# A two-block transformer kernel on one core: two further 2 MB weight slots for the expert stages, taken from double buffers and from the scratch of dynamic transfers

## What is computed

```
pg = softmax(h @ router_g);  gi = argmax(pg)              # one of 4 groups
le = (h @ router_e).reshape(t, 4, 8) of group gi
pk, ik = top_k(softmax(le), 2)                            # two experts of 8 in the group
weight = pg[gi] * pk / sum(pk);  expert = gi * 8 + ik
y[token] += weight * ((silu(x @ w1[e]) * (x @ w3[e])) @ w2[e])   # 32 experts, w1, w3: 1024 x 512, w2: 512 x 1024
x = x + gate * y
```

## Time and profile before

| | us |
|---|---|
| median of three runs (2308.2 to 2309.95) | 2309.11 |
| span of the profiled execution, first to last instruction | 2304.8 |
| median less span | 4.3 |
| PE busy in that span | 2107.9 (91%) |
| PE idle before the UP1 and UP3 products, released by a weight transfer, both layers | 56.3 |
| layer 0 expert stage on PE | 1194.5 to 1656.8 |
| layer 1 expert stage on PE | 1819.8 to 2282.5 |

### The profile page before, as it was taken

The page is one execution under the profiler, slowest core; times in us unless marked ns, Lnnn a source line. Parts: engine busy times, 40 slices in busy tenths (PEclk is TensorE's granted clock), DMA queues, the critical chain, the costliest instruction groups (busy, mean ns, idle before and its releaser), DMA issues. The chain is left out here.

```text
span 2304.8 us, 25911 instructions
## 1 busy us (share of the span) xinstructions
PE 2107.9 (91%) x10718; PEld 1359.1 (59%) x10718; DVE 623.4 (27%) x1420; ACT 461.7 (20%) x899; POOL 252.8 (11%) x385
## 2 busy tenths in 40 slices
PE   8999899999999998878889998888889899998897
PEld 6854587678878755667674443333478644333334
DVE  4566340232213235743231110011111311111101
ACT  2222231222213345444320000000111200000001
POOL 2034120111112133000100000000000001000000
PEclk9999999999999999989889999999899899999998
DMA  7479644334432221110269999999924699999994
GB/s 251 146 325 412 249 146 146 109 128 146 146 99 73 74 73 37 37 38 2 110 248 380 428 428 427 427 427 428 380 100 154 280 379 427 428 428 427 428 428 188
DMA packets 105042, 575.51 MB, mean 250 GB/s; under 512 B 5536, under 2 KB 28665, under 8 KB 75225
## 3 DMA queue, kind: packets, MB, share of 16 engines
q1 hardware_dynamic: 103455, 570.59, 61.6%
q10 hardware_dynamic: 970, 2.23, 0.3%
q0 software_dynamic: 496, 0.97, 0.2%
HBM read 572.72 MB, written 1.05 MB: 249 GB/s over the span
## 5 line engine op out<-in xcount | busy, mean ns | idle before, releaser
L3094 PE MATMUL ex_u<-ring,ex_xt 128*64 128x512 f32 x1024 | 235.1, 614 | 29.2 <-DMA ring<-in_w 27.8
L3094 PE MATMUL ex_u<-ring_extra,ex_xt 128*64 128x512 f32 x1024 | 233.5, 610 | 28.5 <-DMA ring_extra<-in_w 28.5
L784 PE MATMUL linear_ps<-hT,ring 128*128 128x256 f32 x960 | 211.8, 383 | 8.5 <-PEq L444 6.4
L784 PEld LDWEIGHTS linear_ps<-hT,ring 128*128 128x128 f32 x960 | 184.4, 193 | 35.5 <-issue 8.5
L3094 PEld LDWEIGHTS ex_u<-ring,ex_xt 128*64 128x64 f32 x1024 | 82.6, 141 | 178.2 <-issue 178.1
L3094 PEld LDWEIGHTS ex_u<-ring_extra,ex_xt 128*64 128x64 f32 x1024 | 80.5, 141 | 178.7 <-issue 178.1
L2151 PE MATMUL dl_front<-dn_src,ring 128*128 128x256 f32 (+1 forms) x512 | 176.5, 501 | 2.4 <-DVE dp_cv L2318 2.4
L3200 DVE TENSOR_TENSOR ex_hid<-ex_sil,ex_u 128x512 f32<-128x512 f32 x32 | 34.8, 1086 | 490.0 <-PE ex_u L3094 490.0
L1570 PE MATMUL ffn_ps<-hT,ring 128*128 128x256 f32 x704 | 153.9, 382 | 4.3 <-PEq L677 4.3
L1570 PEld LDWEIGHTS ffn_ps<-hT,ring 128*128 128x128 f32 x704 | 134.9, 192 | 23.3 <-issue 4.7
L2151 PEld LDWEIGHTS dl_front<-dn_src,ring 128*128 128x128 f32 x512 | 99.4, 199 | 65.1 <-issue 57.6
(11 more groups left out here) (617 smaller groups left out, 2679.5 us busy)
## 6 DMA issues: line engine op xcount, KB each, us to landing
ring_extra<-in_w SPq DMA_DIRECT2D x88, 2048.0 KB, 25.4
ring<-in_w SPq DMA_DIRECT2D x88, 2048.0 KB, 25.5
ring<-in_ada_w SPq DMA_DIRECT2D x16, 2048.0 KB, 15.9
ring<-in_ffn_w_up SPq DMA_DIRECT2D x22, 1024.0 KB, 6.5
ring<-in_w_in SPq DMA_DIRECT2D x8, 2048.0 KB, 9.2
ring<-in_ada_w SPq DMA_DIRECT2D x16, 1024.0 KB, 14.7
ring<-in_w_in_a SPq DMA_DIRECT2D x8, 2048.0 KB, 8.5
ring<-in_w SPq DMA_DIRECT2D x16, 1024.0 KB, 7.2
```

The costliest lines, as they stand in the source:

```text
L784: mm = pe.matmul(ps[:, q % banks, 0:n], w[:, k, j * P:(j + 1) * P], src[:, k, 0:n], start=k == 0, stop=k == kc - 1)
L3094: mm = pe.matmul(u[H * a:H * a + H, i, :], xt[:, b, k, H * a:H * a + H], cols, start=k == 0, stop=k == KC - 1, skip_group_check=True)
```

## The change

1. `LATE = 2`: two more slots, ten in all, in the expert stages only. `late_slots` allocates them inside `stage_experts`, so their first tiles can be issued once that stage has begun. The list of slots for the experts goes round ten slots in place of eight.
2. SBUF for them: `xt`, `give`, `back`, `ys` get one buffer each; `sil` goes (silu is written into `hid`, in the order that the transposes read, and the multiply works on `hid` in place); `iota` is 128 wide and not 512; `pick` holds two tiles of 128 and not all four, and DVE subtracts 128 from `route_at` ahead of a further tile.
3. With single buffers some waits move: POOL waits for UP3 of the pair before (it was the one before that); ACT's silu waits for the transposes of the pair before; DVE makes the next pair's `give` right after the turned `give`, and copies `back` only after Y0.
4. `dynamic_dma_scratch_size=1024`: POOL's scratch for transfers is cut, and POOL's small loads move to SP, ahead of the weight tiles that SP issues in those two stages.

```
-        self.slots = RING + EXTRA
+        self.slots = RING + EXTRA + LATE
+    def late_slots(self, ctx):
+        for i in range(LATE):
+            self.ring[RING + EXTRA + i] = self.sb(f"ring_late{i}", [P, SLOT], ctx=ctx)
...
         @block.sync
         def _(sp):
+            if loads:
+                loads(sp)
             K.issue(sp, g0 + tiles)
...
-            pool.dma_start(ld[:, :], io["ssm_log_dt"][0]...)          # and four more, now sp.dma_start in start_loads
-        pool.dma_start(S["wg"][:, :, :], w)                           # and six more, now sp.dma_start in start_loads
...
-                elif at < RING + EXTRA:
+                elif at < K.slots:
                     slot = at
                 else:
-                    slot = min(range(RING + EXTRA), key=lambda i: K.latest[i])
+                    slot = min(range(K.slots), key=lambda i: K.latest[i])
...
-        iota = K.sb("ex_iota", [P, 2 * T], ctx=st)
-        pick = K.sb("ex_pick", [P, TT, 2 * T], ctx=st)
+        K.late_slots(st)
+        iota = K.sb("ex_iota", [P, P], ctx=st)
+        pick = K.sb("ex_pick", [P, 2, TT, P], ctx=st)
-        give = K.sb("ex_give", [P, 2, TT, 2, H], ctx=st)
-        xt = K.sb("ex_xt", [P, 2, KC, 2 * H], ctx=st)
-        sil = K.sb("ex_sil", [P, 512], ctx=st)
+        give = K.sb("ex_give", [P, TT, 2, H], ctx=st)
+        xt = K.sb("ex_xt", [P, KC, 2 * H], ctx=st)
-        back = K.sb("ex_back", [P, 2, T], ctx=st)
-        ys = K.sb("ex_ys", [P, 2, D], ctx=st)
+        back = K.sb("ex_back", [P, T], ctx=st)
+        ys = K.sb("ex_ys", [P, D], ctx=st)
...
-                if p >= 2:
-                    pool.wait_ge(full.sem, step(p - 2, UP3))
+                pool.wait_ge(full.sem, step(p - 1, UP3))
...
-                    act.wait_ge(hidden.sem, hidden.at(p))
-                act.activation(sil[:, :], u[:, 0, :], ACT.Silu)
+                    act.wait_ge(turned.sem, turned.at(p))
+                act.activation(hid[:, :].rearrange("s (k q) -> s q k", k=fc), u[:, 0, :].rearrange("s (q k) -> s q k", k=fc), ACT.Silu)
...
-    nc = bacc.Bacc("TRN2", target_bir_lowering=False, num_devices=1)
+    nc = bacc.Bacc("TRN2", target_bir_lowering=False, num_devices=1, dynamic_dma_scratch_size=1024)
```

More of the change, by code:

```diff
@@ L109, in __init__ @@
         self.own = {n: Counter(ctx.enter_context(nc.semaphore(f"{n}_own_step"))) for n in ("dve", "act", "pool")}
-        self.ring = [self.sb(f"ring{i}", [P, SLOT]) for i in range(RING)] + [None] * EXTRA
+        self.ring = [self.sb(f"ring{i}", [P, SLOT]) for i in range(RING)] + [None] * (EXTRA + LATE)
     def unique(self, name):
@@ L154, in no_extra_slots @@
     def no_extra_slots(self):
-        self.ring[RING:] = [None] * EXTRA
+        self.ring[RING:] = [None] * (EXTRA + LATE)
+    def late_slots(self, ctx):
+        for i in range(LATE):
+            self.ring[RING + EXTRA + i] = self.sb(f"ring_late{i}", [P, SLOT], ctx=ctx)
     def issue(self, sp, done, until=None):
@@ L746, in stage_linear_renorm, with linear_stage @@
     K.used = g0 + (4 if fill else 2)
-def linear_stage(K, src, n_chunks, evac, kc=KC, per_tile=4, n=T, beside=None, token_major=()):
+def linear_stage(K, src, n_chunks, evac, kc=KC, per_tile=4, n=T, beside=None, token_major=(), loads=None):
     nc = K.nc
@@ L1054, in cosines, with start_loads @@
         act.activation(S["cos"][:, :, :], rot[:, :, :], ACT.Sin, scale=turn).then_inc(waved.sem, waved.tick())
+    def start_loads(sp):
+        sp.dma_start(ld[:, :], io["ssm_log_dt"][0].rearrange("(i h) -> i h", h=2)).then_inc(loads.sem, loads.tick())
+        for j, n in enumerate(("ssm_b_re", "ssm_b_im")):
+            sp.dma_start(br[:, j], io[n][0].rearrange("g s c -> (g s) c").rearrange("(i q) c -> q i c", q=P)).then_inc(loads.sem, loads.tick())
+        for j, n in enumerate(("ssm_c_re", "ssm_c_im")):
+            sp.dma_start(cr[:, j], io[n][0].rearrange("g c s -> (g c) s").rearrange("(b r) s -> r b s", r=P)).then_inc(loads.sem, loads.tick())
+    S["start_loads"] = start_loads
     def programs(block):
@@ L1734, in evac @@
                     return act.activation(proj[:, c, :], ps, ACT.Sigmoid, bias=K.col("b_gate", c - 16))
-                linear_stage(K, K.hT, 32, evac, token_major=(2,), beside=lambda st: ssm_params(K, S, st))
+                linear_stage(K, K.hT, 32, evac, token_major=(2,), beside=lambda st: ssm_params(K, S, st),
+                             loads=lambda sp: S["start_loads"](sp))
                 K.ada["ps"], K.ada["t_ps"] = K.ps("ada_ps", [P, 512], banks), K.ps("ada_t", [P, 512], banks)
@@ L1947, in program @@
                 w = io[n][l].rearrange("(k p) n -> p k n", p=P)
-                pool.dma_start(K.routers[:, l, :, c:c + w.shape[2]], w).then_inc(loads.sem, loads.tick())
+                sp.dma_start(K.routers[:, l, :, c:c + w.shape[2]], w).then_inc(loads.sem, loads.tick())
+    def program(pool):
         own = K.own["pool"]
@@ L3026, in _ @@
                     for i, part in enumerate((sorted_lo, sorted_hi)):
-                        ins = pool.tensor_copy(xt[:, p % 2, 4 * i:4 * i + 4, H * a:H * a + H], part[:, :, bass.ds(start, H)])
+                        ins = pool.tensor_copy(xt[:, 4 * i:4 * i + 4, H * a:H * a + H], part[:, :, bass.ds(start, H)])
                 ins.then_inc(windowed.sem, windowed.tick())
@@ L3179, in make_give @@
                         e = 2 * p + a
-                        ins = dve.tensor_scalar(give[:, p % 2, t, a, :], iota[:, 0:H], R["place"][:, t, e:e + 1], R["weight"][:, t, e:e + 1],
+                        ins = dve.tensor_scalar(give[:, t, a, :], iota[:, 0:H], R["place"][:, t, e:e + 1], R["weight"][:, t, e:e + 1],
                                                 ALU.is_equal, ALU.mult)
@@ L3204, in _ @@
                 dve.wait_ge(given_turned.sem, given_turned.at(p + 1))
-                dve.tensor_copy(back[:, p % 2, :], g_ps[:, 0:T]).then_inc(back_moved.sem, back_moved.tick())
+                if p + 1 < pairs:
+                    make_give(p + 1)
                 if p + 2 < tiles:
                     make_pick(p + 2)
-                if p + 2 < pairs:
-                    make_give(p + 2)
+                dve.wait_ge(full.sem, step(p, Y0))
+                dve.tensor_copy(back[:, :], g_ps[:, 0:T]).then_inc(back_moved.sem, back_moved.tick())
                 dve.wait_ge(full.sem, step(p, Y1))
-                dve.tensor_copy(ys[:, p % 2, 512:1024], u[:, 1, :]).then_inc(y1_moved.sem, y1_moved.tick())
+                dve.tensor_copy(ys[:, 512:1024], u[:, 1, :]).then_inc(y1_moved.sem, y1_moved.tick())
             for c in range(KC):
```

59 lines of the change are left out of this document (31 added, 28 removed).

## The result

The changed kernel took a median of **2283.36 us** (four runs, 2281.46 to 2292.64) against 2308.65 us for the kernel before on the same chip: a ratio of 0.9897, 95% interval 0.9875 to 0.992. Five further runs of the same kernel gave 2284.98 us, 0.9909 [0.9895, 0.9924].

A forecast was written before the change was run, and what follows sets the result against it. The prediction took the expert stages' weight stream as the bound. Two slots save 2 x 9.8 = 19.6 us, other terms 0: span 2304.8 to 2285.2 us, plus 4.3 gives a median of 2289.5 us; 8-in-10 range 2285.6 to 2299.

The forecast's parts named there:

- The bound: In both expert stages weight transfers at 427 to 428 GB/s set the pace; PE is faster by 4.3 us a pair.
- The two slots: At each expert stage's start two more tiles fill 9.8 us of idle transfer time; each stage ends 9.8 us earlier.
- second gap in layer 0: Idle transfers from 1225 to 1231, 5.3 us; 2.8 us of it would be filled, its end set by PE.
- The marker for PE's waits: PE's wait for tiles over both layers would fall from 56.3 us by somewhat under 20 us.
- Phase of the end: A slower product group after idling may fall behind a stage's last tile: 1.7 us either way per layer, 3.4 us in all.
- The first wait: PE's first wait for a tile in an expert stage would come about two pairs later (9.8 / 4.3).
- The single buffers: POOL, DVE and ACT steps in the expert pairs stay covered by other work; 0 to 1.0 us in all, taken as 0.
- The small loads on SP: S5 tables queued among SP's first weight tiles: between -0.5 and +14.4 us, taken as 0; delta and router loads cost nothing.
- Rival A: Small tables in SP's queue stall PE before the S5 products by up to 14.4 us: up to 2303.9 us; chance 0.12.
- lower bound of -0.5 us: Best case for moving the S5 tables to SP's queue: PE's 0.49 us wait before the S5 products is gone.
- the sum: Both expert stages' gains, -2 x 9.8 = -19.6 us, taken off the 2304.8 us span: 2285.2 us; median 2289.5 us.
- the rest behind the last awaited tile: PE work at each expert stage's end, claimed unchanged, so each stage ends the full 9.8 us earlier.

The follow-up runs named there:

- e_sb8: The changed kernel with LATE = 0 (eight slots), all other edits kept, against the kernel before: median 2305.39 us, ratio 0.9985 [0.9972, 0.9998].

## Why the forecast was right in sign and too high in time

**The bound** held: 426 to 428 GB/s in both stages, PE waits for tiles to the last or last but one pair. The 358 GB/s that the Trainium skill gives for one core ("DMA: Bandwidth & Descriptors", section Specifications) stand there as half of a stack's 716 GB/s, shared by two cores; here one core runs, and the rows show 426 to 428.

**The two slots: right.** -9.8 and -10.3 us by the stages (-9.5 to -10.6 over the four pairs of profiles), against -9.8 each. The prediction's second gap in layer 0 was a little wider than its rows (6.4 us with the stretch behind them, not 5.3), and layer 1 had one too (6.3 us); neither touches the sum, since what limits it is the two tiles. The marker for PE's waits was mis-sized: they fell by 13.4 us, not by just under 20, since 6.7 us came from products that no longer start after a wait. "Phase of the end" had these slow groups as chance of both signs; their sum over a stage falls with the waits. The first wait came two pairs later, as said:

```profile
1424.30 7.09 PE L3109 MATMUL ex_u<-ring,ex_xt 128*64 128x512 f32 x32 [0.89 <-DMA ring<-in_w]
```

Tiles land 27 to 32 us after issue, not 35: the queue grew by one tile on the average, not by two.

**The single buffers: right at nothing, once for a wrong reason.** I expected the multiply into `hid` to take 1.07 us or more, because it "now reads one operand in the strided order". It became faster. Multiply and silu, from the page before:

```profile
L3200 DVE TENSOR_TENSOR ex_hid<-ex_sil,ex_u 128x512 f32<-128x512 f32 x32 | 34.8, 1086 | 490.0 <-PE ex_u L3094 490.0
...
L3153 ACT ACTIVATE ex_sil<-ex_u 128x512 f32<-128x512 f32 x32 | 19.1, 597 | 315.0 <-PE ex_u L3094 315.0
```

From the page after:

```profile
L3221 DVE TENSOR_TENSOR ex_hid<-ex_hid,ex_u 128x512 f32<-128x512 f32 x32 | 22.0, 688 | 471.0 <-PE ex_u L3109 471.0
...
L3168 ACT ACTIVATE ex_hid<-ex_u 128x512 f32<-128x512 f32 x32 | 33.9, 1058 | 314.6 <-PE ex_u L3109 314.6
```

The multiply took 1086 ns before; it had read `sil` in strided order, and now reads `hid` in the order in which it writes. The stride has moved to ACT's write (597 ns before, 1058 after), which lies beside the whole w3 product. I had read the operands the wrong way round. The rule on double buffers of the Trainium skill ("Trainium Kernel Development and Optimization", section Best Practices) did not bite here: every single buffer had other work over it, and `e_sb8` is no slower than before.

**The small loads on SP: right.** DVE has the last S5 table at 25.88 us (before 29.83), and PE's S5 products start at 32.48 without a wait:

```profile
25.88 0.21 DVE L1112 COPY ssm_ldr<-ssm_ld 16x128 f32<-16x128 f32 x1 [8.66 <-DMA ssm_cr<-in_ssm_c_im]
```

```profile
32.48 1.09 PE L1037 MATMUL ssm_ps<-ident,ssm_cx 128*128 128x128 f32 x8
```

Rival A is out: PE's wait is gone, and the price lay below the lower bound of -0.5 us. By 218 us that 1.2 us is gone again.

**The step that failed** is the sum: it took the two stages' gain over into the time as if nothing between and behind them could move, with the words "the rest behind the last awaited tile is PE work that does not change". The scatter does not change, but behind it stands a branch, and 9.9 us of idle PE; that row was in the trace of before, at the very place where the gain had to be handed on, and I did not ask what ended it. It shrank by 5.8 us, because the branch found its piece of program (0.49 us in place of 6.30), and pulled 1.3 us of slow norm products with it. In the span the miss is 24.1 - 19.6 = 4.5 us (7.1 and some smaller gains, less the 3.5 of the dip); the other 1.6 us of the 6.1 come from taking the median 4.3 us above the span; after, it lies 2.7 us above it. An execution's own time is some 1.7 us above its span wherever both are on record (2282.45 against 2280.7), so the rest of the 4.3 must be that the profiled execution of before was quicker than the median. The range had no room for either: single executions of one kernel differ by some 11 us (2281.46 to 2292.64), more than the 3.9 us that it allowed downwards.

What stays open: why PE's fetch comes before the branch in one kernel and not in the other. Shown is that it is not the number of slots alone, not the cut of the program alone, and not chance from one execution to the next, as far as three of each can tell. That the change came with the quick branch was luck: with 128 to 256 more instructions on PE it is gone, with transfers held back the kernel before has it too. The dip that costs the changed kernel 3.5 us in most executions is as little explained.

## What to carry to other kernels

When a stream is full and PE keeps up, look for the stretch where the transfers stand still, and count how many tiles of buffer it is worth: the two slots were worth two tiles a stage, to within a microsecond. Before adding such a gain to the time, follow it across the next barrier: read every idle row between the stage and the next long work, and ask what ends it. And give a change that alters the program a few microseconds of range for each branch that engines wait at, since fetches of the program may fall differently in code that the change never touches.

## What the runs showed of the hardware that I had not expected

- A branch on PE over 117 products (as the program counts them) costs 0.45 to 0.49 us where the piece of program behind it is there, 3.5 to 3.9 us where it must be fetched with no other transfer in flight (layer 1), and 4.2 to 6.4 us where it is fetched among a full weight stream (layer 0). The piece starts 1.0 to 1.5 us after the branch in the second case and 1.7 to 3.8 us after it in the third; the 2.3 to 2.8 us behind that are the same in both.
- Which of these a kernel has can change with 128 instructions added behind the branch (0.49 to 6.40 us), or with transfers held back ahead of it (6.30 to 0.49), or with one slot more (6.30 to 0.49).
- An elementwise instruction on 128 x 512 float32 numbers takes 1058 ns in place of 597 on ACT when it writes in strided order, and 688 in place of 1086 on DVE once its SBUF operand is read in order.
- Five tables of 64 and 256 byte pieces on the queue of the weights were there some 4 us sooner than on POOL's (DVE's first use at 25.88 us, before 29.83).
